# Two-layer hybrid decoder, one core: the first two tiles behind three of the norms are multiplied with the raw residual instead of the normalized one

## The reference

```
x <- LN(a*x + 0.5*SwiGLU_1(x))                          # norm 0
x <- LN(a*x + W_out [RG-LRU | GLA | ConformerConv](x W_in))  # norm 1
x <- LN(a*x + CrossAttn(x, mem))                        # norm 2
x <- LN(a*x + 0.5*SwiGLU_2(x))                          # norm 3
LN(z) = (z - mean(z)) * rsqrt(var(z) + eps) * g + b      # over the features of a position
SwiGLU(x) = (silu(x W_gate) * (x W_up)) W_out           # 2816 hidden features
```

## Time and profile before

| | |
|---|---|
| median of 3 runs | 2272.57 us (2271.89 to 2272.77) |
| profiled execution | 2275.68 us, span 2273.9 us |
| TensorE matmuls | 2199.4 us busy, 97% of the span |
| VectorE, ScalarE, GpSimd | 46%, 34%, 44% busy |
| mean granted TensorE clock | 0.991 of full |

### The profile page before, as it was taken

The page is one execution under the profiler, slowest core; times in us unless marked ns, Lnnn a source line. Parts: engine busy times, 40 slices in busy tenths (PEclk is TensorE's granted clock), DMA queues, the critical chain, the costliest instruction groups (busy, mean ns, idle before and its releaser), DMA issues. The chain is left out here.

```text
span 2273.9 us, 26494 instructions
## 1 busy us (share of the span) xinstructions
PE 2199.4 (97%) x10932; PEld 1818.7 (80%) x10932; DVE 1044.4 (46%) x1108; ACT 783.4 (34%) x1066; POOL 998.8 (44%) x416
## 2 busy tenths in 40 slices
PE   7999999999999899999999999999999998999997
PEld 6888888788787788888878888887786887888886
DVE  2433234787735433332433332257877354333334
ACT  3322224735443422221333222246355334222223
POOL 5444444436432544444444444444265335444442
PEclk9999999999999999999999999999999999999999
DMA  4333322333322233332222333223243212333321
GB/s 165 100 95 96 111 99 56 86 101 103 111 84 65 66 100 95 96 114 92 72 91 93 102 96 114 87 65 84 84 118 105 83 65 70 98 94 101 111 90 50
DMA packets 96041, 210.89 MB, mean 93 GB/s; under 512 B 39344, under 2 KB 52016, under 8 KB 95664
## 3 DMA queue, kind: packets, MB, share of 16 engines
q1 hardware_dynamic: 93536, 205.55, 29.0%
q10 hardware_dynamic: 2384, 3.64, 0.5%
HBM read 207.06 MB, written 2.10 MB: 92 GB/s over the span
## 5 line engine op out<-in xcount | busy, mean ns | idle before, releaser
L468 POOL TENSOR_TENSOR w_lo<-raw,w_hi 128x1024 fp32r<-128x1024 f32 (+2 forms) x358 | 929.1, 2597 | 1228.2 <-ACT w_hi L1120 1228.0
L1120 ACT ACTIVATE w_hi<-raw 128x1024 fp32r<-128x1024 f32 (+2 forms) x358 | 401.5, 1122 | 1319.1 <-PE psum L553 1237.5
L547 PE MATMUL psum<-act_hi,w_hi 128*128 128x512 f32 x1840 | 726.1, 395 | 10.6 <-ACT w_hi L1120 4.1
L550 PE MATMUL psum<-act_lo,w_hi 128*128 128x512 f32 x1840 | 719.9, 391 | 0.0
L553 PE MATMUL psum<-act_hi,w_lo 128*128 128x512 f32 x1840 | 454.5, 389 | 0.0
L547 PEld LDWEIGHTS psum<-act_hi,w_hi 128*128 128x128 f32 x1840 | 347.6, 189 | 89.1 <-ACT w_hi L1120 4.7
L550 PEld LDWEIGHTS psum<-act_lo,w_hi 128*128 128x128 f32 x1840 | 347.8, 189 | 74.4 <-issue 2.4
L553 PEld LDWEIGHTS psum<-act_hi,w_lo 128*128 128x128 f32 x1840 | 345.3, 188 | 71.8
L1583 DVE TENSOR_TENSOR work<-work,psum 128x512 f32<-128x512 f32 x88 | 60.5, 688 | 611.4 <-PE psum L553 561.2
L547 PE MATMUL psum<-h_hi,w_hi 128*128 128x512 f32 x616 | 243.4, 395 | 0.0
L550 PE MATMUL psum<-h_lo,w_hi 128*128 128x512 f32 x616 | 243.1, 395 | 0.0
(11 more groups left out here) (250 smaller groups left out, 2130.3 us busy)
## 6 DMA issues: line engine op xcount, KB each, us to landing
raw<-w_in SPq DMA_DIRECT2D x176, 512.0 KB, 3.5
raw<-w_out SPq DMA_DIRECT2D x64, 704.0 KB, 4.0
raw<-w_kv SPq DMA_DIRECT2D x32, 512.0 KB, 3.5
raw<-w_mix SPq DMA_DIRECT2D x26, 512.0 KB, 3.6
raw<-w_q SPq DMA_DIRECT2D x16, 512.0 KB, 3.6
raw<-w_o SPq DMA_DIRECT2D x16, 512.0 KB, 3.5
raw<-w_v SPq DMA_DIRECT2D x4, 768.0 KB, 4.1
raw<-w_mix SPq DMA_DIRECT2D x24, 128.0 KB, 3.2
```

What stands on the lines that cost most here:

```text
L468: nc.gpsimd.tensor_tensor(w_lo[:, n % SPLIT, 0:width], raw[:, n % RAW, 0:width], w_hi[:, n % SPLIT, 0:width].bitcast(F32), ALU.subtract).t ...
L547: nc.tensor.matmul(o, hi, b_hi, start=start and k == 0, stop=False)
L550: nc.tensor.matmul(o, hi, b_lo, start=False, stop=False)
L1120: A(w_hi[:, n % SPLIT, 0:width], raw[:, n % RAW, 0:width], ACT.Copy).then_inc(w_hi_made, 1)
```

## The change

It touches three kinds of boundary: behind norms 0 and 2 of both layers and behind norm 3 of layer 0.

- As each residual tile is added, ScalarE multiplies it with the gain into a hi operand (`raw_hi`) and VectorE makes its lo operand (`raw_lo`). Two more columns of each row hold gain and bias, so a row has 514 elements.
- `raw_pair` multiplies the first two tiles with these raw operands, each half in a bank of its own, with the two columns beside half b. `stats_rest` for half b is in it after k = 5.
- When the tiles are read, ScalarE copies products and column sums out (`sums_of`) and VectorE brings in mean and scale (`normed_sums`); the bias sum enters in SiLU's bias or in another VectorE instruction.
- `second_pair` makes tiles three and four from the normalized x: tile three by halves, tile four full width. ScalarE's order in the norm is `scaled_later`, which also makes the weight copies for both; GpSimd does both of their splits inside the norm.
- The normalized x is written to another buffer (`NORMED`), as the raw operands are still being read. Behind norms 0 and 3 ScalarE copies it back to `act_hi` and `act_lo` (`returned`), and the tile that needs it waits for `x_returned`. Behind norm 2 the raw operands have the other buffer.
- The banks of an FFN's tiles are swapped where it begins with a raw pair, and in the mixer VectorE clears `SCORES` after `x_returned` instead of ahead of the short convolution.

```diff
+        z2_hi = overlay("z2_hi", 4 * SEQ, [P, KT, ROW])[:, :, :]
+        z2_lo = overlay("z2_lo", 4 * SEQ + KT * ROW, [P, KT, ROW])[:, :, :]
+        x0_hi = overlay("x0_hi", 28 * SEQ, [P, KT, SEQ])[:, :, :]
+        x0_lo = overlay("x0_lo", 36 * SEQ, [P, KT, SEQ])[:, :, :]
+        x3_hi = overlay("x3_hi", 6 * SEQ, [P, KT, SEQ])[:, :, :]
+        x3_lo = overlay("x3_lo", 14 * SEQ, [P, KT, SEQ])[:, :, :]
...
+        act_hi, act_lo = acts_hi[:, :, 0:SEQ], acts_lo[:, :, 0:SEQ]
+        RAW_Z = {0: (acts_hi, acts_lo), 2: (z2_hi, z2_lo), 3: (acts_hi, acts_lo)}
+        NORMED = {0: (x0_hi, x0_lo), 1: (act_hi, act_lo), 2: (act_hi, act_lo), 3: (x3_hi, x3_lo)}
+        sums = small[:, 0:4]
+        minus_sums = small[:, 4:6]
...
             def after_norm(layer, s, x_layer, n):
                 split(layer, s)
-                split_x(x_layer, n, 0, 0)
                 split(layer, s + 1)
-                for h in range(2):
-                    for k in range(0 if h else 2, KT, 2):
-                        split_x(x_layer, n, h, k)
+                for k in range(0, KT, 2):
+                    split_x(x_layer, n, 0, k)
+                split(layer, s + 2)
+                for k in range(0, KT, 2):
+                    split_x(x_layer, n, 1, k)
+                split(layer, s + 3)
...
-                    pe.wait_ge(x_split, x_count(x_layer, n, k + 1, h))
-
-                a, b = HALVES
+            def raw_pair(layer, s, x_layer, n):
+                z_hi, z_lo = RAW_Z[n]
+                def half(j, h, between=None):
+                    r = ring(layer, s + j)
+                    cols = slice(HALF, ROW) if h else HALVES[0]
+                    o = psum[:, 2 * j + h, 0:HALF + 2 * h]
+                    for k in range(KT):
+                        pe.wait_ge(raw_hi_made, raw_part(x_layer, n, k, h))
+                        nc.tensor.matmul(o, weight(r, k)[0], z_hi[:, k, cols],
+                                         start=k == 0, stop=False)
+                        nc.tensor.matmul(o, weight(r, k)[1], z_hi[:, k, cols],
+                                         start=False, stop=False)
+                        pe.wait_ge(raw_lo_made, raw_part(x_layer, n, k, h))
+                        last = nc.tensor.matmul(o, weight(r, k)[0], z_lo[:, k, cols],
+                                                start=False, stop=k == KT - 1)
+                        if between and k == 5:
+                            between()
+                    return last
+                slot_ready(layer, s)
+                half(0, 0, lambda: stats_rest(x_layer, n, 1))
+                half(0, 1).then_inc(slot_multiplied, 1)
+                slot_ready(layer, s + 1)
+                half(1, 0)
+                half(1, 1).then_inc(slot_multiplied, 1)
+            def second_pair(layer, s, outs, x_layer, n):
+                x_hi, x_lo = NORMED[n]
+                def hi_by_hi(h):
+                    cols = HALVES[h]
+                    for k in range(KT):
+                        pe.wait_ge(x_hi_made, x_count(x_layer, n, k // 2 * 2 + 1, h))
+                        nc.tensor.matmul(outs[0][:, cols], weight(ring(layer, s), k)[0],
+                                         x_hi[:, k, cols], start=h == 0 and k == 0, stop=False)
+                def lo_by_hi(h):
+                    cols = HALVES[h]
+                    for k in range(KT):
+                        nc.tensor.matmul(outs[0][:, cols], weight(ring(layer, s), k)[1],
+                                         x_hi[:, k, cols], start=False, stop=False)
+                def hi_by_lo(h):
...
+                pe.wait_ge(raw_sums_read, 2 * raw_norm(x_layer, n) + 1)
+                for h in range(2):
+                    hi_by_hi(h)
+                    if h == 0:
+                        hi_by_lo(0)
+                        slot_ready(layer, s)
+                    lo_by_hi(h)
+                hi_by_lo(1).then_inc(slot_multiplied, 1)
+                tile_of(layer, s + 1, outs[1], lambda k: (x_hi[:, k, :], x_lo[:, k, :]), KT)
...
+                    outs = [bank(hidden_bank(layer, f, i, g)) for g in range(2)]
+                    if raw and i == 1:
+                        second_pair(layer, s, outs, *raw)
+                        return
+                    if raw and i == 2:
+                        pe.wait_ge(raw_sums_read, 2 * raw_norm(*raw) + 2)
+                    elif i >= 2:
                         pe.wait_ge(gate_silu, base + i - 1)
                         pe.wait_ge(h_made, base + i - 1)
+                    if raw and not f and i == 3:
+                        pe.wait_ge(x_returned, 2 * layer)
+                    operand = normed if raw and not f and i == 2 else act
                     for g in range(2):
...
+                    if (kind, i) == ("ca", 0):
+                        pe.wait_ge(raw_sums_read, 2 * raw_norm(layer, 0) + 2)
+                    if (kind, i) == ("ca", 1):
                         pe.wait_ge(xc_ready, layer * AT + AT)
-                    tile_of(layer, S_MIX + MIX_SLOT[kind, i], bank(MIX_BANK[kind, i]), act, KT)
+                    if (kind, i) == ("k", 0):
+                        pe.wait_ge(x_returned, 2 * layer + 1)
+                    tile_of(layer, S_MIX + MIX_SLOT[kind, i], bank(MIX_BANK[kind, i]),
+                            normed if (kind, i) == ("ca", 0) else act, KT)
...
-                first_pair_by_halves(layer, S_MIX, layer, 0)
-                project("xa", 2)
-                project("cg", 0)
+                raw_pair(layer, S_MIX, layer, 0)
+                second_pair(layer, S_MIX + 2, [bank(0), bank(1)], layer, 0)
...
+            def raw_hi(layer, n, m, cols):
+                c = V_LN + 16 * n
+                z_hi = RAW_Z[n][0]
+                if m == 0:
+                    A(z_hi[:, :, SEQ:ROW],
+                      vecs[:, c:c + 2 * KT].rearrange("p (w k) -> p k w", w=2), ACT.Copy)
+                A(z_hi[:, m, cols], x[:, m, cols], ACT.Identity,
+                  scale=vec(c + m)).then_inc(raw_hi_made, 1)
...
+            def scaled_later(layer, n, next_s, square_b, to):
+                hi = NORMED[n][0]
+                def affines(h, k):
+                    affine(layer, n, k, HALVES[h])
+                    affine(layer, n, k + 1, HALVES[h])
+                def copied(h, k):
+                    cols = HALVES[h]
+                    A(hi[:, k:k + 2, cols], x[:, k:k + 2, cols], ACT.Copy).then_inc(x_hi_made, 2)
+                def sums_of(j):
+                    act.wait_ge(slot_multiplied, next_s + j + 1)
+                    o = to(j)
+                    A(sums[:, 2 * j:2 * j + 2], psum[:, 2 * j + 1, HALF:HALF + 2], ACT.Copy)
+                    A(o[:, HALVES[0]], psum[:, 2 * j, HALVES[0]], ACT.Copy)
+                    A(o[:, HALVES[1]], psum[:, 2 * j + 1, HALVES[0]],
+                      ACT.Copy).then_inc(raw_sums_read, 1)
+                square_of_mean(layer, n, 0)
+                root(layer, n, 0)
+                w_hi_of(next_s)
+                affines(0, 0)
+                affines(0, 2)
+                square_b()
+                w_hi_of(next_s + 1)
+                if n != 2:
+                    act.wait_ge(slot_multiplied, next_s)
+                act.drain()
+                copied(0, 0)
+                copied(0, 2)
+                square_of_mean(layer, n, 1)
+                affines(0, 4)
+                root(layer, n, 1)
+                affines(0, 6)
+                act.drain()
+                copied(0, 4)
+                copied(0, 6)
+                for k in range(0, KT, 2):
+                    affines(1, k)
+                    act.drain()
+                    copied(1, k)
+                    if k == 0:
+                        sums_of(0)
+                        w_hi_of(next_s + 2)
+                    if k == 4:
+                        w_hi_of(next_s + 3)
+                sums_of(1)
+                silu_table()
...
+            def returned(n, parts):
+                for part in parts:
+                    back, k = (act_hi, act_lo)[part // 4], part % 4 * 2
+                    last = A(back[:, k:k + 2, :], NORMED[n][part // 4][:, k:k + 2, :], ACT.Copy)
+                return last
...
                 for i in range(FT):
+                    if raw and i == 0:
+                        act.wait_ge(raw_normed, raw_norm(*raw) + 1)
+                        A(work[:, 0, :], work[:, 0, :], ACT.Silu,
+                          bias=sums[:, 1:2]).then_inc(gate_silu, 1)
+                        continue
                     w_hi_of(s0 + 2 * i + SPLIT)
                     if i >= 2:
                         act.wait_ge(h_made, base + i - 1)
-                    A(work[:, i % 2, :], bank(2 * (i % 2)), ACT.Silu).then_inc(gate_silu, 1)
+                    if raw and not f and i == 1:
+                        act.wait_ge(x_split, x_count(*raw, KT - 1, 1))
+                        returned(3, range(0, 4))
+                    A(work[:, i % 2, :], bank(hidden_bank(layer, f, i, 0)),
```

(113 more changed lines are left out.)

141 lines of the change are left out of this document (43 added, 98 removed), and 2 rows, old and new, of the table MIX_STEPS.

## The result

The kernel after takes 2280.64 us (median of 6 runs, 2278.24 to 2284.44) against 2272.32 us before (6 runs, 2271.72 to 2273.09): a ratio of 1.0038, interval 1.0028 to 1.0049. It is slower by 8.3 us; the prediction had it faster by 17.7. The profiled execution took 2280.98 us, its span is 2279.1.

The account below looks back on a forecast made before the run. TensorE, busy 97% of the span, bounds the kernel, so only its waits and lowered clock can yield. Boundaries 23.5 - attention output 1.6 - clock 4.2 = 17.7 us faster: 2255 us, own range 2249 to 2261, overall 2240 to 2268.

Parts of the forecast that it names:

- rival E: Rows of 514 elements lose alignment; 3.2 ns on TensorE's 1840 matmuls of each of three kinds undo 17.7 us; chance 0.02.
- last sign of being wrong: Wrong altogether if the raw pair exceeds 13 us behind norm 0, or full-width matmuls are slower than now.
- the two extra columns: Gain and bias columns in the raw pair's matmuls: under 1 ns each, taken as 0.
- Boundaries: From T, the preceding output tile's end, to tile four's end, at five norms: 23.5 us gained in sum.
- wait before the last `x_hi`: In tile three behind norm 0, TensorE arrives at T+16.3 and waits 2.0 us for ScalarE.
- the chain: Norm 0's steps, summed plainly: variance ends T+5.4, first scaled pair T+8.7, last `x_hi` T+18.3.
- Rival B: Norm chain: variance instruction meets a whole GpSimd split, chain 1.6 us later per boundary, clock falls stay: 2267 us; chance 0.22.
- Behind norm 2: TensorE starts 0.5 us late, `stats_rest` waits 1.4 us, four tiles done at T+29.5: gain 4.3 us, twice.
- Behind norm 3: Layer 0: copies for tiles three and four precede the loads, tile five's is 0.7 us late: gain 7.5 us.
- Attention output: VectorE's extra subtraction delays the second tile's addition, whose bank tile four needs: 0.8 us a layer, 1.6 in all.
- The clock: The new 2.0 us waits may lower TensorE's clock; half of five falls of 1.7 us charged: 4.2 us.
- rival D: Copies back hold ScalarE ahead of weight copies at three places, up to 8.5 us each: slower, 2280 us; chance 0.09.

Follow-up runs that it names:

- sixth run: The kernel after with act rows 576 elements (2304 bytes) apart instead of 514: 2251.22 us, ratio 0.9902.
- seventh: The kernel after with act rows 576 elements apart and a pad of 160 bytes ahead of the shared region: 2234.63 us, ratio 0.9833.
- third run: The kernel before with pads ahead of `act_hi` and behind `act_lo`, moving act by 32 bytes and `w_hi` by 128: 2312.3 us, ratio 1.0174.
- fourth run: The kernel before with a pad of 8 elements (32 bytes) ahead of the shared region, `h_hi` at 134400: 2273.13 us, ratio 0.9998.

## Why the prediction was wrong

**The step that failed** is rival E. It named the event ("rows of 514 elements start off their old alignment"), counted the readers (1840 of each of three kinds) and worked out that 3.2 ns each would undo the gain. Then it was given 0.02, on the strength of a row that doesn't bear on it: how fast ScalarE writes an unaligned row. A write by ScalarE says nothing about a read by TensorE. The nearest row for that was on the page and wasn't looked for: the same matmul at 389 ns from `act_hi` and 395 from `h_hi`, whose starts differ by other than a multiple of 256 bytes. By that row the bound of E is 6 ns: 3 x 1744 x 6 = 31 us, which turns a gain of 17.7 into a loss of 14, 2286 us. It measured 5.5 ns and 28.8 us. The prediction's own last sign of being wrong, "full-width matmuls slower than now", is the one that came.

**The sentence "the two extra columns are under 1 ns each; I take 0"** held for what it priced: the raw pair took 12.35 us behind norm 0, forecast 12.4. What the two columns cost was not in the matmuls that read them, but in the 512-wide ones that skip them.

**Boundaries.** Forecast T+26.0, 29.5, 26.8 for the three kinds, measured 25.7, 29.5, 26.2; gains forecast 23.5 in sum, measured 25.2. The wait before the last `x_hi` is 1.56 to 1.61 us, forecast 2.0. Behind norm 0 the chain ran 0.3 to 0.4 us ahead of the sum: the variance ended at T+5.15 (forecast 5.4), the first scaled pair of half b at T+8.4 (8.7), the last `x_hi` was there at T+17.9 (18.3). TensorE got there at T+16.3, as forecast.

**Rival B.** Its sign, a variance TENSOR_SCALAR of over 2 us, did not come: it took 0.59 us. But the event that B names did happen. The same instruction takes 0.29 us where GpSimd does nothing (before, at 374.04), and wherever GpSimd was at work when it began (five times before, five after) it ended 0.15 us after GpSimd's instruction did: 385.45 after 385.30 in the kernel before, 392.78 after 392.63 here. So it was held until the split ended, which agrees with the rule that B names. What differs is how late in the split it came, 1.55 us before the end then, 0.44 now. The sum had it right, with the split ending at T+5.2 and the variance at T+5.4; B's whole split would have needed the two to begin together.

The first row is of the kernel before, the others of the kernel after.

```profile
382.93 2.37 POOL L468 TENSOR_TENSOR w_lo<-raw,w_hi 128x1024 fp32r<-128x1024 f32 x1 [2.04 <-ACT w_hi L1120]
...
390.23 2.40 POOL L522 TENSOR_TENSOR w_lo<-raw,w_hi 128x1024 fp32r<-128x1024 f32 x1 [3.68 <-ACT w_hi L1183]
...
392.19 0.59 DVE L1700 TENSOR_SCALAR var<-var 128x256 f32<-128x256 f32 x1
...
395.38 0.69 DVE L1740 TENSOR_TENSOR x<-x,psum 128x512 f32<-128x512 f32 x1
```

Behind norm 2, `stats_rest` waits 1.18 us (forecast 1.4) and the start 0.48 (forecast 0.5); the raw pair ends at T+15.7 (15.3) and the last `x_hi` is there at T+21.7 (21.8). Behind norm 3, the 3.17 us wait is gone and 0.35 stands before tile five (forecast 0.7): the loads are issued behind both weight copies, as the prediction ordered them.

**Attention output.** Charged 0.8 us a layer, measured 0.92 and 0.93, at tile four as named.

**The clock.** Charged 4.2 us, half of five falls; none of the five boundaries shows one in the profiled execution (1.00 in all windows above). Its mean granted clock rose from 0.991 to 0.997, and the profiled executions of the sixth and seventh runs have 0.997 too. The five waits of 1.6 us were not followed by a fall to 1.2 GHz. So this term was 4.2 us too large. The Trainium skill ("TensorE: Matmul & The Clock Gate", Part 1), by which nothing was charged, gave the better number. The kernel before doesn't bear it out as a rule: behind norm 2 of layer 1 the clock fell (0.93) with no wait over 1.81 us, hardly longer than these five.

**Copies back (rival D).** ScalarE's eight copies are there (3.89 us for four, twice, behind norm 3), with weight copies between. D would have shown as waits for `w_hi` or `evac` in the tiles after tile four; in the 30 us behind it there is one, the 0.35 us above, which comes before the copies back, and behind norm 0 of both layers none.

```profile
1165.21 3.89 ACT L1320 ACTIVATE acts_hi<-x_hi 128x1024 fp32r<-128x1024 f32 x4
1169.00 0.57 ACT L1339 ACTIVATE work<-psum 128x512 f32<-128x512 f32 x1
1169.48 1.04 ACT L1183 ACTIVATE w_hi<-raw 128x1024 fp32r<-128x1024 f32 x1
1170.43 3.89 ACT L1320 ACTIVATE acts_lo<-x_lo 128x1024 fp32r<-128x1024 f32 x4
```

In the prediction's own terms: the boundary terms, summed without the clock's charge, give 23.5 - 1.6 = 21.9 us faster, and the sixth run, which is the change without E, is 20.8 us faster. What decided was one term, E, put at nothing; the clock's charge, 4.2 us too much, erred the other way and made the miss look smaller.

## What to carry to other kernels

When a change alters the row length or the place of a buffer that TensorE streams, treat it as a change to every matmul that reads the buffer, and look on the page for the same instruction form reading from two places: a few ns between them, times the count, can exceed all waits. Compare the distances of starts, as one pass of three showed nothing in its durations here. In kernels of 512-wide fp32r matmuls, put moving rows and weights a multiple of 256 bytes apart (pad the row, pad ahead of the tensor), and both at a multiple of 128, where all fast operands here stood; here that was worth 29 us in one operand and 13 to 17 us in another, for one line each. A bound for an unknown cost must come from a row of the engine and the direction in question.

## What the runs showed of the hardware

- The distance between 512-wide fp32r matmuls depends on where the moving row starts relative to the weights: 226.7 to 227.5 ns at multiples of 256 bytes, 229.4 at 64 past one, 232 to 234 at 32, 96, 128, 160 (third run) and 192, 236.8 at 4. Both shifted together: 238.0 ns at 4 bytes, 230.1 at 16, 227.7 to 228.8 at 32 to 256. At 256 columns it doesn't (119.9 unshifted, 118.0 shifted by 32), at 384 hardly (173.6 and 173.3).
- VectorE's TENSOR_SCALAR on 256 fp32 columns took 0.29 us alone; begun during a GpSimd subtraction, it ended 0.15 us after that one, in ten of ten cases, and so took 0.59 to 1.70 us.
- The Trainium skill ("SBUF — State Buffer", "A bandwidth-pool intuition that's wrong") gives TensorE's weight loads a read port of their own and calls contention in SBUF structural only. The runs fit that poorly: with all other engines idle, moving the weights alone by 128 bytes costs 5.5 ns a matmul. That weights are read while rows stream would explain it; no run here separates that from other causes.
- The same skill ("TensorE: Matmul & The Clock Gate", Part 1) has 512 columns at 215.7 ns start to start at the higher clock. No tile of 24 came below 226.6 ns on average; fp32r tiles that change weights each time run at 226.7 at best.
- Single distances go by a pattern that differs with the address: for h they are 231, 232 and 237 ns in turn in the kernel before (96 bytes past a multiple of 256 from the weights) and 237 and 229 in turn in the fourth run (128 past); the mean is 233.3 to 233.4 in both. Why is open.
